# Wide late up-products, low halves on GpSimd and two-tensor one-hot rows in an expert layer

## What is computed

```python
u = u_tab[ix]                                   # rows of the chosen experts
act = gelu(einsum('chkd,cd->chk', u, hx))       # "up": one number per chosen expert
vv = v_tab[ix]
out = einsum('chk,chkd->cd', gx * act, vv)      # "down": gated sum
```

## Time and profile before

| what | value |
|---|---|
| three runs | 1875.52, 1877.52, 1877.57 us |
| span of the profiled execution, first to last instruction | 1874.2 us |
| granted TensorE clock, mean over the span | 0.989 |
| TensorE busy | 1824.1 us (97%) |
| VectorE busy | 1305.0 us (70%) |
| ScalarE busy | 922.9 us (49%) |
| GpSimd busy | 116.3 us (6%) |

### The profile page before, as it was taken

The page is one execution under the profiler, slowest core; times in us unless marked ns, Lnnn a source line. Parts: engine busy times, 40 slices in busy tenths (PEclk is TensorE's granted clock), DMA queues, the critical chain, the costliest instruction groups (busy, mean ns, idle before and its releaser), DMA issues.

```text
span 1874.2 us, 30697 instructions
## 1 busy us (share of the span) xinstructions
PE 1824.1 (97%) x12639; PEld 1677.6 (90%) x12639; DVE 1305.0 (70%) x2098; ACT 922.9 (49%) x1238; POOL 116.3 (6%) x75
## 2 busy tenths in 40 slices
PE   7999899999999999999999999999999999989998
PEld 7999899999999999988888888888888889878887
DVE  5567875999788888755555557887577445757744
ACT  6447635444344343444444445766455343546533
POOL 0000002670000000000000000030000000100000
PEclk9999999999999999999999999997999999989999
DMA  6444345454444443465555553421155456625543
GB/s 236 162 159 161 132 180 204 168 188 170 153 155 147 146 158 137 160 232 193 189 200 186 195 197 124 148 83 64 65 183 179 178 200 221 175 96 206 186 169 145
DMA packets 44757, 310.66 MB, mean 166 GB/s; under 512 B 5182, under 2 KB 5694, under 8 KB 8160
## 3 DMA queue, kind: packets, MB, share of 16 engines
q1 hardware_dynamic: 42592, 303.58, 44.9%
q0 software_dynamic: 1472, 4.86, 1.4%
q10 hardware_dynamic: 576, 0.55, 0.1%
HBM read 306.84 MB, written 2.13 MB: 165 GB/s over the span
## 4 chain that ended last, share of the span: by engine, by line
PE 69%; DVE 12%; ACT 2%; issue 1%; POOL 0%; ACTq 0%; DVEq 0%
PE bank L347 20%; PE bank L1706 18%; PE bank L3034 9%; PE bank L358 6%; PE bank L362 3%; PE bank L1677 3%; PE bank L3293 2%; DVE s_arena L1846 1%; DVE s_ring_lo L310 1%; PE bank L446 1%; PE bank L2659 1%; DVE s_arena L1843 1%; DVE s_arena L1889 1%; DVE s_arena L2121 1%; PE bank L2597 1%
## 5 line engine op out<-in xcount | busy, mean ns | idle before, releaser
L310 DVE TENSOR_TENSOR s_ring_lo<-s_ring,s_w_hi 128x2048 fp32r<-128x2048 f32 x227 | 519.7, 2290 | 173.1 <-ACT s_w_hi L304 168.6
L304 ACT ACTIVATE s_w_hi<-s_ring 128x2048 fp32r<-128x2048 f32 x244 | 465.8, 1909 | 132.1 <-PE bank L347 42.3
L347 PE MATMUL bank<-s_h_r,s_w_hi 128*128 128x256 f32 x3072 | 405.2, 285 | 0.3 <-DVE s_arena L3522 0.3
L347 PEld LDWEIGHTS bank<-s_h_r,s_w_hi 128*128 128x128 f32 x3072 | 381.7, 192 | 4.8 <-issue 3.6
L1706 PE MATMUL bank<-s_w_hi,s_h_r 128*128 128x512 f32 x1008 | 238.8, 389 | 0.3 <-issue 0.3
L1706 PEld LDWEIGHTS bank<-s_w_hi,s_h_r 128*128 128x128 f32 x1008 | 189.2, 188 | 39.6 <-issue 0.4
L347 PE MATMUL bank<-s_h_r,s_ring_lo 128*128 128x256 f32 x1536 | 215.7, 283 | 1.4 <-DVE s_ring_lo L310 1.4
L347 PEld LDWEIGHTS bank<-s_h_r,s_ring_lo 128*128 128x128 f32 x1536 | 198.1, 192 | 1.8 <-DVE s_ring_lo L310 1.8
L1806 ACT ACTIVATE s_h_r<-s_arena 128x512 fp32r (+1 forms) x64 | 40.4, 632 | 184.6 <-PE bank L1706 184.6
L3006 DVE TENSOR_TENSOR s_ring_lo<-s_ring,s_spare_r 128x2048 fp32r<-128x2048 f32 x32 | 73.1, 2291 | 78.6 <-ACT s_spare_r L2992 78.6
L1706 PE MATMUL bank<-s_ring_lo,s_h_r 128*128 128x512 f32 x504 | 124.5, 389 | 0.0
(11 more groups left out here) (464 smaller groups left out, 2501.3 us busy)
## 6 DMA issues: line engine op xcount, KB each, us to landing
s_ring<-weights SPq DMA_DIRECT2D x282, 1024.0 KB, 4.8
s_arena<-bias_by_distance POOLq DMA_DIRECT2D x12, 384.0 KB, 7.9
s_arena<-mem SPq DMA_DIRECT2D x1, 1024.0 KB, 5.7
s_x<-x SPq DMA_DIRECT2D x1, 1024.0 KB, 13.4
x_away<-s_x SPq DMA_DIRECT2D x1, 1024.0 KB, 7.9
s_arena<-sub_keys SPq DMA_DIRECT2D x1, 1024.0 KB, 11.0
s_arena<-x_away SPq DMA_DIRECT2D x1, 1024.0 KB, 8.4
out<-s_x SPq DMA_DIRECT2D x2, 512.0 KB, 2.6
```

What stands on the lines that cost most here:

```text
L304: act.activation(k.w_hi[:, u % 2, :], k.ring[:, u % RING, :], ACT.Copy).then_inc(k.hi_ready, 1)
L310: dve.tensor_tensor(k.ring_lo[:, u % RING, :], k.ring[:, u % RING, :], plain(k.w_hi[:, u % 2, :]), ALU.subtract).then_inc(k.lo_ready, 1)
L347: last = pe.matmul(out[:, nb * S:(nb + 1) * S], w[:, c, nb * P:(nb + 1) * P], h[:, c, :], start=(n == 0 and c == 0), stop=(n == 2 and c == 7))
```

## The change

Late units get another form of product. The high half of the weights is multiplied with both halves of the tokens in one matmul of 512 columns, and the low half with the high half of the tokens into the second half of the same bank. Each 128-expert half of a unit has a bank of its own, `ps[0]` and `ps[1]`, the same for all late units. ScalarE copies the first half of a bank into a buffer of 256 columns, `across` (`cross`), and VectorE adds that to the second half and writes the sum to `ps[2 + j % 2]` (`join`), where `gelu` then works. There is one buffer `across`, so the second `cross` waits for the first `join`. `spread` has four banks in place of six.

The low halves of units 22 to 64 (43 instructions of 128x2048) go from VectorE to GpSimd. The four one-hot instructions of `heat` become `scalar_tensor_tensor`, with the gate as a second tensor. In VectorE's list `heat(g+1)` comes first in a group, and `join` last; in ScalarE's, `cross` comes last.

```diff
+def unit_T_banks(k, pe, u, h_hi, h_swapped, banks, half_done, free):
+    hi, lo = unit_parts(k, u)
+    split_ready(k, pe, u, 0)
+    for nb in range(2):
+        free(nb)
+        for c in range(8):
+            pe.matmul(banks[nb][:, :], hi[:, c, nb * P:(nb + 1) * P], h_swapped[:, :, c, :], start=(c == 0), stop=False)
+        if nb == 0:
+            split_ready(k, pe, u, 2)
+        for c in range(8):
+            last = pe.matmul(banks[nb][:, S:2 * S], lo[:, c, nb * P:(nb + 1) * P], h_hi[:, c, :],
+                             start=False, stop=(c == 7))
+        if nb == 0:
+            last.then_inc(half_done, 1)
     last.then_inc(k.unit_done, 1)
...
-    bank = [ps[2 + g % 6] for g in range(GROUPS)]
+    bank = [ps[4 + g % 4] for g in range(GROUPS)]
...
+            def free(nb):
+                if j == EARLY_R:
+                    pe.wait_ge(gelu_out, EARLY_R - 1 + nb)
+                else:
+                    pe.wait_ge(summed, 2 * (j - 1 - EARLY_R) + nb + 1)
+
+            unit_T_banks(k, pe, split_unit(j), k.hT_hi, h_swapped, ps[0:2], half_done, free)
...
-            if g >= 6:
-                pe.wait_ge(spread_out, g - 5)
+            if g >= 4:
+                pe.wait_ge(spread_out, g - 3)
...
+            act.wait_ge(summed, 2 * (j - EARLY_R + 1))
+            act.activation(ps[2 + j % 2][:, :], ps[2 + j % 2][:, :], ACT.Gelu_apprx_tanh).then_inc(gelu_out, 1)
...
+        def cross(j):
+            for nb in range(2):
+                if nb == 0:
+                    act.wait_ge(half_done, j - EARLY_R + 1)
+                else:
+                    act.wait_ge(k.unit_done, F + j + 1)
+                if j > EARLY_R or nb:
+                    act.wait_ge(summed, 2 * (j - EARLY_R) + nb)
+                act.activation(across, ps[nb][:, 0:S], ACT.Copy).then_inc(crossed, 1)
...
             if g >= 1:
                 copy(g - 1)
+            if g in up_at:
+                cross(up_at[g])
...
-        for u in range(Q + 2, F + POOL_R):
+        for u in (*range(Q + 2, F + POOL_R), *range(F + EARLY_R + 2, F + PAIRS + 1)):
             n = u - k.whole_units
             pool.wait_ge(k.hi_ready, n + 1)
             pool.wait_ge(k.lo_ready, n)
...
-                dve.tensor_scalar(hot[:, g % 2, 0, n, :], k.iota, i1, gate, ALU.is_equal, ALU.mult)
+                dve.scalar_tensor_tensor(out=hot[:, g % 2, 0, n, :], in0=k.iota, scalar=i1,
+                                         in1=gate.to_broadcast([P, KEYS]), op0=ALU.is_equal, op1=ALU.mult)
...
+        def join(j):
+            for nb in range(2):
+                dve.wait_ge(crossed, 2 * (j - EARLY_R) + nb + 1)
+                dve.tensor_tensor(ps[2 + j % 2][:, nb * S:(nb + 1) * S], ps[nb][:, S:2 * S], across,
+                                  ALU.add).then_inc(summed, 1)
...
         for g in range(GROUPS + 1):
+            if g + 1 < GROUPS:
+                heat(g + 1)
             if g in up_at and up_at[g] > EARLY_R:
                 combine(up_at[g] - 1, max(g - 1, 0))
-                split_lo(k, dve, split_unit(up_at[g] + 1))
             if g >= 1:
                 multiply(g - 1)
-            if g + 1 < GROUPS:
-                heat(g + 1)
+            if g in up_at:
+                join(up_at[g])
...
+            if d == 0:
+                dve.wait_ge(k.lo_ready, F + PAIRS + 1 - k.whole_units)
```

More of the change, by code:

```diff
@@ L348, in unit_T_split @@
                                  start=(n == 0 and c == 0), stop=(n == 2 and c == 7))
+    last.then_inc(k.unit_done, 1)
+def unit_T_banks(k, pe, u, h_hi, h_swapped, banks, half_done, free):
[12 more added lines that the diff above has]
+            last.then_inc(half_done, 1)
     last.then_inc(k.unit_done, 1)
@@ L1595, in peer @@
     x_back = carve(k, 0, TT, D)
-    names = ("keys_here", "q_out", "score_mm", "score_out", "shift_ready", "exp_ready",
-             "chosen_ready", "chosen_turned", "slots_ready", "h_split", "gelu_out", "hot_ready", "spread_mm",
+    names = ("keys_here", "q_out", "score_mm", "score_out", "dve_prepared", "act_prepared", "half_done", "crossed", "summed",
+             "chosen_ready", "chosen_turned", "slots_ready", "gelu_out", "hot_ready", "spread_mm",
              "multiplied", "spread_out", "combined", "weighted_round", "weighted_ready", "bank_done",
[L1599 to L1602, removed]
+             "query_scaled")
+    (keys_here, q_out, score_mm, score_out, dve_prepared, act_prepared, half_done, crossed, summed, chosen_ready, chosen_turned,
+     slots_ready, gelu_out, hot_ready, spread_mm, multiplied, spread_out, combined, weighted_round,
+     weighted_ready, bank_done, query_scaled) = (ctx_sem(k, n) for n in names)
     own = k.steps
@@ L1610, in peer @@
     up_at = up_turns()
-    bank = [ps[2 + g % 6] for g in range(GROUPS)]
+    bank = [ps[4 + g % 4] for g in range(GROUPS)]
+    H_SPLIT, SHIFTED = 1, 2
+    QUERY_SPREAD, EXPS = 1, 2
+    across = k.joined[:, :]
+    h_swapped = k.h_r[:, 0:2]
     def present(g):
@@ L1650, in score @@
             if h == 1:
-                pe.wait_ge(query_spread, 1)
+                pe.wait_ge(act_prepared, QUERY_SPREAD)
             if h >= 2:
@@ L1665, in up @@
                 pe.wait_ge(q_out, PEER_H)
[L1666 removed]
+            elif j < EARLY_R:
                 pe.wait_ge(gelu_out, j - 1)
[L1668 to L1670 removed]
+            if j < EARLY_R:
+                unit_T_split(k, pe, split_unit(j), *h_pair, ps[j % 2])
+                return
+            def free(nb):
[4 more added lines that the diff above has]
+            unit_T_banks(k, pe, split_unit(j), k.hT_hi, h_swapped, ps[0:2], half_done, free)
         def spread(g):
             pe.wait_ge(hot_ready, g + 1)
[L1674 to L1675 removed]
+            if g >= 4:
+                pe.wait_ge(spread_out, g - 3)
             for n in range(GROUP_T):
@@ L1725, in tensor @@
         score(PEER_H - 1)
-        pe.wait_ge(h_split, 1)
+        pe.wait_ge(dve_prepared, H_SPLIT)
         for j in range(EARLY_R):
@@ L1765, in scalar @@
                 act.wait_ge(k.turned, 4 * k.norms + 1)
-                act.activation(begin.spread, ps[3][:, 0:S], ACT.Copy).then_inc(query_spread, 1)
+                act.activation(begin.spread, ps[3][:, 0:S], ACT.Copy).then_inc(act_prepared, 1)
             if h == 2:
@@ L1771, in gelu @@
         def gelu(j):
-            act.wait_ge(k.unit_done, F + j + 1)
-            out = flat(k.G[:, 2 * j:2 * j + 2, :]) if j < EARLY_R else ps[j % 2][:, :]
-            act.activation(out, ps[j % 2][:, :], ACT.Gelu_apprx_tanh).then_inc(gelu_out, 1)
+            if j < EARLY_R:
+                act.wait_ge(k.unit_done, F + j + 1)
+                act.activation(flat(k.G[:, 2 * j:2 * j + 2, :]), ps[j % 2][:, :], ACT.Gelu_apprx_tanh)\
+                   .then_inc(gelu_out, 1)
+                return
+            act.wait_ge(summed, 2 * (j - EARLY_R + 1))
+            act.activation(ps[2 + j % 2][:, :], ps[2 + j % 2][:, :], ACT.Gelu_apprx_tanh).then_inc(gelu_out, 1)
         def copy(g):
@@ L1869, in vector @@
         factor()
-        dve.wait_ge(query_spread, 1)
+        dve.wait_ge(act_prepared, QUERY_SPREAD)
         for n in range(KC):
@@ L1879, in vector @@
                 dve.wait_ge(k.x_saved, 16)
-                dve.tensor_tensor(k.x_r[:, :], flat(scaled), plain(flat(k.hT_hi)), ALU.subtract).then_inc(h_split, 1)
+                dve.tensor_tensor(k.x_r[:, :], flat(scaled), plain(flat(k.hT_hi)), ALU.subtract).then_inc(dve_prepared, 1)
             dve.wait_ge(score_out, h + 1)
@@ L1895, in vector @@
         first = top[:, :, :, 0:1].to_broadcast([P, TT, PEER_H, TOPK])
-        dve.tensor_tensor(shifted, top, first, ALU.subtract).then_inc(shift_ready, 1)
+        dve.tensor_tensor(shifted, top, first, ALU.subtract).then_inc(dve_prepared, 1)
         for n, (amount, op) in enumerate(((4, ALU.logical_shift_right), (2, ALU.logical_shift_right),
@@ L1939, in vector @@
                 own.settle(dve)
-        dve.wait_ge(exp_ready, 1)
+        dve.wait_ge(act_prepared, EXPS)
         own.up(dve.tensor_reduce(total, shifted, AX.X, ALU.add))
@@ L1979, in combine @@
             dve.wait_ge(gelu_out, j + 1)
-            act, at = halves(ps[j % 2][:, :]), k.G[:, 2 * j:2 * j + 2, :]
+            act, at = halves(ps[2 + j % 2][:, :]), k.G[:, 2 * j:2 * j + 2, :]
             if t:
@@ L3682, in build @@
         k.small = sb("small", [P, 64])
-        k.gdn_small = sb("gdn_small", [P, 7, 4, GDN_H])
+        k.joined = sb("joined", [P, S])
+        k.gdn_small = k.joined[:, 0:7 * 4 * GDN_H].rearrange("p (a b c) -> p a b c", a=7, b=4)
         k.half_b = sb("half_b", [P, 48])
```

5 lines of the change are left out of this document (3 added, 2 removed).

## The result

The changed kernel takes 1963.68 us (median of 4 runs, 1960.39 to 1966.84), the kernel before beside it 1876.74: ratio 1.0464 [1.0447, 1.0482], 87 us slower. The profiled execution took 1960.39 us, with a span of 1958.6.

A forecast was written before the change was run, and what follows sets the result against it. TensorE was taken to bound the late part, at 14.18 us per turn; with the change, 21.5 turns of 19.2 us add 108 us, plus 0.9 behind the last unit, giving 1987 us, range 1915 to 2010.

The forecast's parts named there:

- The mechanism: Late part: GpSimd's low halves hold one-hots and get in between them, VectorE's queue waits behind; 1987 us, chance 0.68.
- The expected signs: Late part: 43 low halves of 4.63 us on GpSimd, about two long one-hots per turn, one of 4 to 5 us.
- Heat isn't held: Late part: one-hots run through GpSimd's time, TensorE sets the turn at 13.83 us; 1871 us, chance 0.05.
- Perfect packing: Late part: heats and low halves fit outside each other without gaps, 14.87 us per turn; 1893 us, chance 0.06.
- The sum: Late part: one turn's steps in sequence, 19.57 us, 19.2 after overlaps; over 21.5 turns 412.8 us, 108 more than before.
- the one-hot's price: VectorE's heat: 0.32 us per new-form one-hot, bounds 0.28 and 0.45, making 1.87 us per group.
- the held heat: VectorE beside GpSimd: third heat lets in the next low half, then finishes after it: 4.63 + 1.87 = 6.50 us.
- The 0.9 us behind the last unit: End of the late part: a cross and a join, 0.85 us, come before the first down.
- the 3.3 us around the span: Outside the profiled span: 3.3 us added to the span of 1983, as in the median before.
- TensorE's part: Late units: wide matmuls take 5.58 us instead of 5.75; 13.83 us per turn, at most 7.5 us won over 21.5 turns.
- The clock: TensorE in the late part: full granted clock expected, though busy only 13.83 of 19.2 us per turn.
- the rival's mechanism: Late part: TensorE's clock falls to the lower level in a tenth of the turns, adding 18 us; 2005 us, chance 0.05.

The follow-up runs named there:

- the best kernel: Changed kernel with iota row in PSUM, ScalarE's high half ahead of gelu, first half's join ahead of multiply and spread copy: 1871.69 us, 0.9973.
- the run with both orders and the hold left in: Changed kernel, iota in SBUF, low halves on GpSimd, with high half ahead of gelu and first half's join early: 1934.87 us, 1.0313.

## Why the prediction was right

**The mechanism** is the one forecast as the likeliest. One-hot rows in the new form are held while GpSimd works; GpSimd gets its next low half in between two of them; combine, multiply and join queue behind; TensorE waits, 1.3 us at most at a time. The expected signs were there: 43 low halves of 4.6 us in the late part, and four one-hots in 7.76 us beside four in 1.13. *Heat isn't held* is excluded by the held one-hots and by the kernel with a PSUM operand. *Perfect packing* fell to the queues, as argued.

**The sum** gave 1987 for 1963.68. Read from one turn by the starts of its steps, forecast in brackets: heat 1.65 (1.87), multiply 0.50 (0.53), copy 0.23 (0.32), gelu 0.52 (0.52), high half 1.98 (1.93), from the first low half to the end of the held heat 10.37 (4.63 + 6.50 = 11.13), combine 0.85 (0.75), multiply 0.52 (0.53), copy 0.23 (0.32), cross 0.41 (0.40), join 0.53 (0.45), cross 0.42 (0.40), join 0.34 (0.42). Together 18.55 against 19.57 less 0.36. Two terms are too large:
- the one-hot's price. I took 0.32 and gave 0.28 as the lower bound; the spacing in a free heat is (1.13 - 0.34) / 3 = 0.26, that of the old form. The range of the price did not hold it.
- the held heat. I let all of it stand outside the low halves. Two low halves took 9.43 us and only 10.37 - 9.43 = 0.94 of the heat came behind them: a held one-hot ends with the low half that held it (each of the 41 long ones within 0.16 us behind it), and the rest got in between.

That is 0.66 us in a turn, 14 us in 21.5 turns; the first two turns were also shorter (15.5 and 18.1 us, from the start of a unit to the start of the one after the next). The late part was forecast to take 413 us and took 394.8. The 0.9 us behind the last unit came as 1.5, and the 3.3 us around the span as 1.8 (1960.39 less 1958.6). The stretch behind, which I took as unchanged, was 6 us shorter in the profiled execution, at a granted clock of 0.99 against 0.98; why it was is open.

**TensorE's part** was sized right: without any wait its turn is two units of 5.67, the single spread's 0.81 and the pair's 1.71, 13.86 us, for 13.83 forecast. These are read from start to start, from end to end, which shifts some time between unit and spread. Start to start a unit of the kernel before took 648.58 - 642.75 = 5.83 us:

```profile
642.75 2.16 PE L347 MATMUL bank<-s_h_r,s_w_hi 128*128 128x256 f32 x16
...
648.58 1.06 PE L1677 MATMUL bank<-s_hT 128*128 128x128 f32 x8
```

So a wide unit saves 0.16 us, for 0.17 forecast. Of the 7.5 us the best kernel shows some 5.

**The clock** was forecast as full and was not. At 654.71 eight matmuls took 3.47 us where eight took 2.09 in other units. The granted clock in that piece, and in the 4.71 us ahead of it, where TensorE was busy 2.44:

```profile
650.00:654.71 4.71, 2.44 (x21) 2.09 (x19) 3.78 (x7) 0.66 (x3) 1.18 (x1) 1.00 0.62 223
654.71:657.98 3.27, 3.27 (x9) 2.58 (x10) 2.90 (x9) 0.74 (x3) 0.00 (x0) 0.55 0.02 5
```

0.55 is near the lower of the two levels, 1.2 of 2.4 GHz. So the rival's mechanism came once in this turn, behind a stretch with gaps, but not its price: that half was over when the second half's matmuls of 659.15 followed, and its cross started only at 660.71, behind gelu and high half. It is so in the other turns: from the third on, eleven have a granted clock of 0.91 to 0.98 and take 18.30 to 18.84 us, and the eight at 1.00 take 18.48 to 18.66. TensorE was busy 328.5 of 394.8 us, 83%, where 72% were forecast. The turn was shorter, and slow matmuls count as busy, but that is not all: in the run with both orders and the hold left in, at a granted clock of 1.00 from the first spread to the last, TensorE is recorded busy for 311 us with matmuls that take 295 in the fastest kernel. So work that is broken up by waits is recorded longer too.

## What to carry to other kernels

Before work is moved to GpSimd beside VectorE, list which of VectorE's instructions read only SBUF, and where they stand in its list: the price is not the held time (157 us held cost 30 in one order, 129 cost 82 in the other) but what queues behind it. One operand in PSUM took the hold away for the price of a bank. Where three engines hand a unit round in a ring, an order that is harmless with slack becomes the bound; put first what the bounding engine waits for next, and look at the ring again after each step, since each cure here uncovered the next wait.

## What was not expected of the hardware

- The one-source compare and multiply (TENSOR_SCALAR, 128x128 float32) was held by GpSimd up to 4752 ns, like the two-tensor form. Unlike it, it sometimes kept GpSimd waiting: four low halves recorded with 5.27 to 5.30 us instead of 4.6.
- The two-tensor form costs the same per one-hot as the one-source form, 0.26 us, though it reads a second tensor. With the iota row in PSUM its median stays at 342 ns (345 in the changed kernel), while that of the one-source form goes from 341 to 402.
- The granted clock fell within a turn behind 4.71 us in which TensorE was busy for 2.44, and in the kernel with low halves on VectorE too (0.57 from 648.13 to 651.27, behind 3.63 us with 1.02 busy).
